# A merge of two variants of a three-block kernel: VectorE's turn order, divisions by two heads, router and first expert reordered, gates' products moved, output stored in pieces

## What is computed

```python
for ly in range(2):                     # first block: two hybrid layers
    proj = x @ w_in                     # q, k, v, z_attn, z_ssm, xbc, dt
    attn = window_attention(q, k, v, sinks) * silu(z_attn)
    ssm = gated_rmsnorm(ssd(silu(conv(xbc)), dt), z_ssm)
    x = layer_norm(ALPHA * x + concat(attn, ssm) @ w_out)
h = x + mixer(rmsnorm(x))               # second block: conv and attention branch
u = rmsnorm(h)
logits = u @ [w_group, w_router]        # 8 groups, 64 experts
g = argmax(group logits); two best of the group's 8 experts, softmax weights
h = h + sum_e weight_e * (silu(u @ w1[e]) * (u @ w3[e])) @ w2[e]
gate, scale, shift = c @ w_ada + b_ada  # third block
n = rms_norm(h) * (1 + scale) + shift
proj = n @ w_in_3                       # cq, ckv, gates, q, k, v, f, mg_a, mg_b
y_a = mla_attention(...) * silu(gate_a); y_b = fox_attention(...) * silu(gate_b)
merged = sigmoid(mg_a) * (y_a @ w_branch_a) + sigmoid(mg_b) * (y_b @ w_branch_b)
out = h + gate * (merged @ w_out_3)
```

## Time and profile before

| | us |
|---|---|
| median of 3 runs | 2007.69 |
| lowest, highest | 2006.94, 2009.26 |
| the profiled execution | 2007.99 |
| its span in the profile | 2006.3 |
| PE busy | 1615.6 (81%) |
| DVE busy | 605.9 (30%) |
| ACT busy | 290.6 (14%) |
| bytes moved by DMA | 553.33 MB, mean 276 GB/s |

### The profile page before, as it was taken

How to read it: one execution, slowest core, us unless ns; L and a number is a source line. 1 busy time by engine, 2 the same in 40 slices (tenths; PEclk the granted TensorE clock), 3 DMA queues, 4 the chain that set the end, 5 groups by cost and what they waited for, 6 DMA issues and landing times.

```text
span 2006.3 us, 20852 instructions
## 1 busy us (share of the span) xinstructions
PE 1615.6 (81%) x9002; PEld 954.5 (48%) x9002; DVE 605.9 (30%) x1386; ACT 290.6 (14%) x781; POOL 11.1 (1%) x35
## 2 busy tenths in 40 slices
PE   9999999999999998856565665655566656898998
PEld 6675567755688885322221222221222221456875
DVE  3663455634242313311110111111111110345432
ACT  0243313432021002000000000000000000122210
POOL 0000000000000000000000000000000000000000
PEclk9999999999999999978777887778887877998999
DMA  9841376433433563899999999999999999734200
GB/s 365 275 123 47 105 265 198 126 108 113 165 126 126 213 249 126 371 427 428 428 428 427 427 427 427 428 427 428 428 427 428 428 427 418 274 127 153 99 0 21
DMA packets 106630, 553.33 MB, mean 276 GB/s; under 512 B 5825, under 2 KB 12481, under 8 KB 82977
## 3 DMA queue, kind: packets, MB, share of 16 engines
q1 hardware_dynamic: 105680, 548.82, 68.9%
q0 software_dynamic: 848, 3.05, 0.4%
HBM read 550.80 MB, written 1.05 MB: 275 GB/s over the span
## 4 chain that ended last, share of the span: by engine, by line
PE 57%; DMA 35%; DVE 4%; ACT 2%; issue 1%; SPq 0%; DVEq 0%
PE bank L631 28%; DMA ring<-in_w 19%; DMA arena<-in_w 14%; PE bank L1077 8%; PE bank L658 6%; PE bank L640 4%; PE bank L1098 3%; PE bank L619 3%; DMA ring<-in_w_ada 1%; PE bank L840 1%; DVE arena L1970 1%; PE bank L772 1%; PE bank L752 1%; DMA prm<-in_pk 0%; DVE sm L2012 0%
## 5 line engine op out<-in xcount | busy, mean ns | idle before, releaser
L631 PE MATMUL bank<-arena,ring 128*128 128x256 f32 x1856 | 415.1, 382 | 0.5 <-DVE arena L2226 0.5
L1077 PE MATMUL bank<-ring,arena 128*32 128x512 f32 x1216 | 284.6, 729 | 147.5 <-DMA ring<-in_w 96.5
L631 PEld LDWEIGHTS bank<-arena,ring 128*128 128x128 f32 x1856 | 351.0, 191 | 50.9 <-issue 2.8
L1077 PE MATMUL bank<-arena 128*32 128x512 f32 x832 | 233.6, 727 | 98.9 <-DMA ring<-in_w 52.9
L631 PE MATMUL bank<-ring,arena 128*128 128x512 f32 (+3 forms) x584 | 233.1, 550 | 2.8 <-DVE arena L2888 1.0
L1077 PEld LDWEIGHTS bank<-ring,arena 128*32 128x32 f32 x1216 | 72.2, 131 | 275.4 <-issue 275.4
L1098 PE MATMUL bank<-ring,arena 128*32 128x512 f32 x608 | 131.6, 678 | 33.4 <-DMA ring<-in_w 23.2
L631 PEld LDWEIGHTS bank<-ring,arena 128*128 128x128 f32 x584 | 108.1, 190 | 100.6 <-issue 87.3
L1077 PEld LDWEIGHTS bank<-arena 128*32 128x32 f32 x832 | 57.7, 131 | 178.6 <-issue 178.5
L1098 PE MATMUL bank<-arena 128*32 128x512 f32 x416 | 108.9, 702 | 27.0 <-DMA ring<-in_w 13.6
L658 PE MATMUL bank<-ring,arena 128*128 128x512 f32 (+1 forms) x320 | 127.3, 555 | 2.6 <-DMA ring<-in_w_vd 1.6
(11 more groups left out here) (374 smaller groups left out, 1316.3 us busy)
## 6 DMA issues: line engine op xcount, KB each, us to landing
ring<-in_w SPq DMA_DIRECT2D x114, 2048.0 KB, 30.5
arena<-in_w SPq DMA_DIRECT2D x78, 2048.0 KB, 30.2
ring<-in_w_in SPq DMA_DIRECT2D x40, 2048.0 KB, 8.1
ring<-in_w_ada SPq DMA_DIRECT2D x6, 2048.0 KB, 13.7
ring<-in_w_out SPq DMA_DIRECT2D x6, 2048.0 KB, 7.8
ring<-in_w_out SPq DMA_DIRECT2D x16, 512.0 KB, 8.3
ring<-in_w_conv_out SPq DMA_DIRECT2D x2, 2048.0 KB, 8.4
ring<-in_w_attn_out SPq DMA_DIRECT2D x2, 2048.0 KB, 8.2
```

The costliest lines, as they stand in the source:

```text
L631: i = te.matmul(ps, lhsT, rhs, start=n0 + k == 0, stop=n0 + k == n - 1)
L1077: m = te.matmul(ps[32 * j:32 * j + 32, :], LM.xg[:, f, 128 * k + 32 * j:128 * k + 32 * j + 32], vs[j][:, 512 * (k % 2):512 * (k % 2) + 512 ...
```

## The change

It joins two variants of this kernel; it has these parts.

1. DVE's steps "proj" stand last in each turn (layers and third block). PE and ACT keep "proj" first.
2. In the layers DVE takes the maxima at the end of the step with the second half of the scores, and in layer 0 a third of the sums for `w_ada` moves from the q steps to the za steps.
3. Router: the arg-maxima run on the raw logits in PSUM, and 1/rms is applied at the end; the last transposed piece is copied by ACT, not DVE; the last transpose and logits stand ahead of the ranks; `group(1)` stands ahead of `scales(1)`.
4. First gather in pieces: token half 0 while DVE still works on half 1; the count stands behind the first quarter of `up`.
5. Each expert group's transposes of the weights `Sw` stand ahead of `down`.
6. The gate products (L1324) move into the last group's `down`, ahead of the last quarter weight, to banks 4 and 5.
7. Third block: `un` in halves of 512 columns; mlaprep one turn earlier at its start and with four steps more (25); squares on ACT; the root's wait is a step of its own; probabilities divided two heads at a time, a transpose group waiting only for its own two; mla from turn 23; vb copies swapped between ACT and DVE.
8. `wo3` starts as merged pieces arrive; its last quarter is two pieces of 256 columns; five stores in place of one.

```diff
-def last_order():
+def last_order(proj_last=False):
-    total = dict(proj=40, foxprep=7, mlaprep=21, fox=34, mla=34)
+    total = dict(proj=40, foxprep=7, mlaprep=25, fox=34, mla=34)
...
-        add("proj", 1)
+        if not proj_last:
+            add("proj", 1)
         add("foxprep", 1)
-        add("mlaprep", 0 if turn < 5 else 2 if 7 <= turn < 11 else 1)
         add("fox", 0 if turn < 7 else 2)
-        add("mla", 0 if turn < 22 else 2)
+        add("mla", 0 if turn < 23 else 2)
+        add("mlaprep", 0 if turn < 4 else 2 if 6 <= turn < 12 else 1)
+        if proj_last:
+            add("proj", 1)
...
# sync_program
-            le.dma_start(out[0].rearrange("(t p) d -> p t d", p=128), h[:, :, :]).then_inc(out_sem, 16)
+            for g in range(2):
+                for tt in range(2):
+                    for o in (0, 256) if g + tt == 2 else (0,):
+                        n0, n = 512 * g + o, 256 if g + tt == 2 else 512
+                        s.wait_ge(*at.of("h", 3, tt, g, o))
+                        le.dma_start(out[0, 128 * tt:128 * tt + 128, n0:n0 + n], h[:, tt, n0:n0 + n]).then_inc(*stored.inc())
...
# tensor_program, mixer_out and experts
                 logits(1, 0)
-                rank = [fresh("rank", tt, b=2 + tt) for tt in range(2)]
...
+                turn_h(1, 1)
+                rank(0)
+                logits(1, 1)
+                rank(1)
...
-                mixer_rank()
-                parts[0][0](0)
+                parts[0][0](0, js=(0,), tts=(0,))
+                rank_second()
+                parts[0][0](0, js=(1,), tts=(0,))
+                parts[0][0](0, tts=(1,))
...
-                    up(f, 0)
+                    up(f, 0, None if g else count)
...
-                    mid_T()
-                    down()
-                    scatter(f)
+                    mid_T(f)
+                    down(gates if g == NG0 - 1 else None)
+                    scatter()
...
# tensor_program, third block
-                    ready(("probs", kind, k))
                     for c2 in range(2):
+                        ready(("probs", kind, k, c2))
...
-                ready(*[("merged", i) for i in range(8)])
...
+                                if g + tt == 0:
+                                    t.wait_ge(*at.of("merged", c))
...
# scalar_program
+                h_turned(1, 1)
                 root(1)
...
+                for tt in range(2):
+                    se.activation(L3.qsq[tt], L3.qa[:, tt, :], ACT.Square).then_inc(*a.done("squares", "q", tt))
+                    se.activation(heads(L3.ksq[tt]), heads(L3.kva[:, tt, :], 128)[:, :, 0:64], ACT.Square
+                                  ).then_inc(*a.done("squares", "k", tt))
+                    yield
...
# vector_program, layers
-                    for _ in range(3):
+                    for _ in range(3 if ly else 2):
                         next(sums)
...
                     gated(("za", ly, i), L1.zaT[:, i, :], 256)
+                    if ly == 0:
+                        next(sums)
...
-                    yield
+                    if g2 == 0:
+                        yield
...
                 ve.tensor_scalar(mx, mx, -1.0, None, ALU.mult).then_inc(*v.done("mx", ly, n))
+                yield
...
-                in_order(layer_order(), ...
+                in_order(layer_order(proj_last=True), ...
# vector_program, router
-                    ve.tensor_scalar(lg[:, tt, :], bank("lg", tt)[:, 0:72], LM.rstd[:, tt:tt + 1], None, ALU.mult
-                                     ).then_inc(*v.done("ev", "lg", tt))
-                    first_max(lg[:, tt, 0:8], tt, oh, gm)
+                    raw = bank("lg", tt)
+                    first_max(raw[:, 0:8], tt, oh, gm)
...
-                v.wait_ge(*at.of("mm", "h2T", 1, 1))
-                ve.tensor_copy(LM.u2[:, 4:8, 128:256], ...
                 places(0)
+                group(1)
                 scales(1)
-                group(1)
                 two(1)
# vector_program, third block
-                    ve.tensor_tensor(t3, q3, q3, ALU.mult).then_inc(*v.step())
...
-                    ve.tensor_tensor(t3, k3, k3, ALU.mult).then_inc(*v.step())
...
+                    v.wait_ge(*at.of("squares", "q", tt))
...
-                        if i % 2:
+                        if i == 1:
                             yield
...
                     ve.tensor_scalar(mx, mx, -scl, None, ALU.mult).then_inc(*v.done("mx", kind, k))
+                    yield
...
-                    ve.tensor_tensor(sc[:, :, 0:nk], sc[:, :, 0:nk], bc(col1(sume), nk), ALU.mult
-                                     ).then_inc(*v.done("probs", kind, k))
+                    for c2 in range(2):
+                        sk = sc[:, 2 * c2:2 * c2 + 2, 0:nk]
+                        ve.tensor_tensor(sk, sk, bc(col1(sume[:, 2 * c2:2 * c2 + 2]), nk), ALU.mult
+                                         ).then_inc(*v.done("probs", kind, k, c2))
...
-                in_order(last_order(), ...
+                in_order(last_order(proj_last=True), ...
```

More of the change, by code:

```diff
@@ L1104, in down, with scatter @@
                                 t.also("used", name)
-                def scatter(f):
-                    ps = take(7, "SwT")
-                    t.wait_ge(*at.of("Sw", *key))
-                    for tt in range(2):
-                        m = te.transpose(ps[:, 128 * tt:128 * tt + 128], LM.Sw[:, f, 128 * tt:128 * tt + 128], ident[:, :])
-                    m.then_inc(*t.done("mm", *tag("SwT")))
+                def scatter():
                     for tt in range(2):
@@ L1243, in mla_prep @@
                         yield
-                for _ in range(7):
+                for _ in range(11):
                     yield
@@ L1340, in last_block @@
                     for tt in range(2):
-                        tok(("wo3", tt, g), L3.mga, weights(("wo3", g)), tt, 512)
+                        last = g + tt == 2
+                        for o in (0, 256) if last else (0,):
+                            n = 256 if last else 512
+                            ps = fresh("wo3", tt, g, o)
+                            for c in range(8):
+                                if g + tt == 0:
+                                    t.wait_ge(*at.of("merged", c))
+                                m = te.matmul(ps[:, 0:n], L3.mga[:, c, 128 * tt:128 * tt + 128],
+                                              weights(("wo3", g))[:, c, o:o + n], start=c == 0, stop=c == 7)
+                            m.then_inc(*t.done("mm", "wo3", tt, g, o))
                         if tt:
@@ L2750, in mla_prep @@
                                      ).then_inc(*v.step())
-                    t3 = heads(tm[:, 0:512])
-                    ve.tensor_tensor(t3, k3, k3, ALU.mult).then_inc(*v.step())
-                    behind()
-                    ve.tensor_reduce(rn[:, 8 * tt:8 * tt + 8], t3, AX.X, ALU.add).then_inc(*v.step())
-                    behind()
+                    v.wait_ge(*at.of("squares", "k", tt))
+                    ve.tensor_reduce(rn[:, 8 * tt:8 * tt + 8], heads(L3.ksq[tt]), AX.X, ALU.add).then_inc(*v.step())
+                    ready(("qkb", "read"), ("ev", "ckv", tt))
                     ve.tensor_tensor(tm[:, 0:32], L3.ckv[:, tt, 256:288], L3.ckv[:, tt, 256:288], ALU.mult
```

193 lines of the change are left out of this document (110 added, 83 removed).

## The result

The changed kernel takes 1972.81 us (median of 4 runs, 1971.79 to 1973.57), the kernel before in the same comparison 2008.47 us (2006.94 to 2012.80). The ratio is 0.9819, with a 95% interval of 0.9802 to 0.9836. The forecast was 1976.0 us and faster, with a range of 1971 to 1985. The profiled execution of the changed kernel took 1971.79 us with a span of 1970.0; against the span before, 2006.3, that is 36.3 us less, where the sum of the prediction had 32.5, less the half it gave back.

What follows compares the result with a forecast made beforehand. Full DMA engines bound the experts' stage; elsewhere PE's waits and the clock falls behind them are on the path. Terms summed to 32.5 us off 2007.99; 0.5 given back made 1976 us, range 1971 to 1985.

Steps and rivals of the forecast that it cites:

- Layers: In the layers, four division waits (4.9 us) and a q copy wait (1.4) go: 6.3 us, between nothing and 6.3.
- Stream: Start of the experts' weight stream: shorter router chain and split gather let the first load issue 3.3 us sooner, range 2 to 5.2.
- full clock: Start of the experts' stream: at full clock the first quarter of `up` would end 5.2 us sooner.
- half clock over gather and quarter: Start of the experts' stream: if half clock covers the new half gather and the quarter of `up`, it ends 2 us sooner.
- End of the experts: Last expert `down` and after: gate products in PE's wait 1.8 us, `Sw` transposed earlier 0.2, `un` in halves 0.3.
- Third block, early: Early third block: waits for log_f, normed latents and a bank shrink, less a new bank wait: 3.1 us, between 1.5 and 3.6.
- The 8.0 us and its clock: Second fox tile, third block: the division wait goes, 8.0 us (5 to 8.0), and half clock behind it, 2.5 (0 to 2.5).
- mla and tail: Third block: mla division waits net 2.1 us and their half clock 1.7; tail (merged pieces, last product, smaller last store) 3.2.
- ScalarE did not become late in the third block: First rival: in the third block the division's wait moves to a late ACT and does not go; 1983.5 us, chance 0.16.
- evictions behind proj cost nothing: Second rival: later proj evictions in the layers make PE wait, so the layers give nothing; 1982 us, chance 0.12.
- slower rival: Late evictions cost PE time in every turn of layers and third block; 2021 us at 0.33 us a turn, chance 0.02.
- The stream did not start as before: Fourth rival: the experts' stream starts as before, gathers waiting for POOL and low clock covering all; 1979 us, chance 0.14.

Runs made afterwards that it cites:

- order undone, and alone: VectorE's proj step first again in the layers of the kernel after: 1981.71 us; only that step put last in the layers of the kernel before: 2001.04 us.
- preparation first: Kernel after with mla's preparation ahead of attention in VectorE's turn in the third block: 1972.53 us.
- maxima late: Kernel after with the third block's maxima one attention step behind the scores and one empty step before the division gone: 1972.61 us.
- proj first: Kernel after with VectorE's proj step first in its turn in the third block only: 1975.32 us.
- squares and division: Kernel after with the four squares back on VectorE and the division in one piece, in the third block: 1974.45 us.
- four together: Kernel after with proj first, mla's preparation ahead of attention, squares on VectorE and division in one piece, all in the third block: 1977.77 us.
- five together: Kernel after, third block: proj first, preparation ahead of attention, squares on VectorE, whole division, and maxima one attention step behind the scores: 1988.87 us.
- runs with fillers: Kernel after with products of 512 columns, results overwritten unread, ahead of the first gather: six took 1973.31 us, three 1970.96 us.
- gates late: Kernel after with gate products behind the third block's first products again, and one 1024 KB store after a last product of 512 columns: 1979.06 us.

## Why the prediction was right, point by point

**Layers**: 6.3 forecast, 7.0 measured, with the reason shown from both sides for the 4.9 (order undone, and alone); the edit of the sums, to which the 1.4 is put down, was not undone by itself. That the two numbers lie so close is partly luck. The waits' price is over what their rows show, 1.4 us here as in the run with the order alone; 0.25 us came from an earlier load of `w_vd`, which varies; and against this stand the two new waits of 0.44 us on ScalarE's copy, which I had not priced. They are in neither run of the order, so the order and the other edits of the layers make them together. In the kernel after the old waits would bring half clock with them.

**Stream**: 3.3 taken of a range of 2 to 5.2, 4.8 measured, and 3.5 to 4.9 by the nine profiles with these instructions. This is the term that was mis-sized most. I chose between "full clock" and "half clock over gather and quarter", and in this profile neither came: half clock lay over the gathers (24 in 4.93 us), full over the quarter (1.92). In three of the nine the 24 took 5.92 us, near my slow case. The rest of the error is the pieces of half 0, which filled two waits, where I had counted one half of the gather as gone and the other at full or half rate.

**End of the experts**: `un` in halves gave 0.3 as forecast (1.38 us of wait, from 1.64). `Sw` gave nothing: the wait ahead of the scatter went from 0.61, for ScalarE, to 0.91, for VectorE's copy of the other half. The gates gave their 1.8, and removed a standstill that can cost 1.5 more.

**Third block, early**: 3.1 forecast. The waits for log_f, the latents and the bank, 3.5 us together, became 0.4, which is the 3.1 forecast. Undoing the order alone brought back 1.8, so the order is not all of it; what the rest is was not tried.

**The 8.0 us and its clock**: 10.5 forecast, and wait and half clock are gone. Here the forecast had the size right and the cause only in part. I wrote that scores, maxima and division at the head of the turn, and four squares less, take the wait away. At this tile each undone alone costs nothing (preparation first, maxima late, proj first) or 0.35 us (squares and division), four together 1.05 us, five together 4.15 and half clock. So no single part is needed, and all that I named bring only half of the 8.0 back. What the change made is cover, 1.7 us at this tile, and each part that is undone uses up some of it. The page "ScalarE: Activation LUTs" of the Trainium skill (section on what a table load costs) has 1.28 us for the load and about 2.7 with the drain; the load took 1.28 here, and the next instruction of ScalarE began 1.30 us after its start, so none of the cover went to a drain.

**mla and tail**: 3.8 and 3.2 forecast. Of the waits only 0.48 us for the last gating is left (0.4 forecast), and no window has half clock. The merged pieces and the tail gave 1.0 + 2.8: the last 128 KB landed in 1.7 us, where I took the 2.3 of a load.

**The rivals.** ScalarE did not become late in the third block: it did the four squares in 2.6 us, from 1800.84 to 1803.47, and was free before the root needs it. PE has no new wait on VectorE in the layers, so evictions behind proj cost nothing that a row shows, and VectorE's order alone made the kernel before faster, which rules out the slower rival there. The stream did not start as before.

## What to carry to other kernels

A wait of 8 us can go by several edits of which no single one is needed, and half of it come back only with five of them undone: count the cover (when the result is there, when it is asked for) rather than crediting each edit, and undo parts together before saying which one was needed. Work that does not depend on the late result belongs in every wait ahead of it, in pieces as small as the waits; pieces of the gather were worth 2 to 3.6 us, and short waits on TensorE also cost through its clock. VectorE's steps that wait for a product of the current turn go last in its turn: that alone gave 6.2 us here.

## What the runs showed of the hardware

The granted clock is not a function of the program alone. In layer 0, from 84 to 96 us, with PE busy for 12.00 of 12.00 us, it was 1.00 in the kernel after and 0.86 in the run with the third block's order undone, whose layers are the same. First the window of the kernel after:

```profile
84.00:96.00 12.00, 12.00 (x75) 9.90 (x72) 8.01 (x19) 1.91 (x5) 0.00 (x0) 1.00 0.42 142
```

Then that of the run with the order undone:

```profile
84.00:96.00 12.00, 12.00 (x64) 9.68 (x61) 6.40 (x17) 1.41 (x4) 0.00 (x0) 0.86 0.42 153
```

The two runs with fillers have 0.86 there too; of the profiles whose layers are those of the kernel after, three of eleven have it, and each loses up to 0.14 x 12 = 1.7 us. What PE does there is the head of the attention, its scores and small products, between stretches of wide ones. So it falls to 1.2 GHz without any standstill in some executions, and after standstills of 2.95 us (kernel before) and 3.20 us (gates late) it did not fall in the one and fell in the other; after the same 1.8 us for log_f it fell with four and with five parts undone and not with the order alone undone. In front of the experts, behind products of 64 to 128 columns, 1.34 us were enough. The first sixteen products of 272 columns, at 7.6 us, took 3.93 us in the kernel after and 5.62 to 5.71 in three others (preparation first, four and five parts undone), whose first product of `wo2` comes 1.0 to 1.1 us later; the granted clock reads 1.00 there, so the cause stays open. Differences of 1 to 2 us between kernels like these are therefore within what executions of the same instructions differ by.
